# The low parts of the second attention's query weights on GpSimd instead of VectorE

## What is computed

```
for i in range(2):
    h = rms_norm(x, mix_norm[i])
    if i == 0: x = x + neighbourhood_attention(h, na_w_qkv, na_rpb, na_w_o)
    else:      x = x + sliding_window_gqa(h, swa_w_qkv, swa_sinks, t5_rel_table, swa_w_o)
    h = rms_norm(x, mlp_norm[i])
    x = x + relu(h @ mlp_w_in[i])**2 @ mlp_w_out[i]
return rms_norm(x, final_norm)
```

```
s = q @ k.T + bias            # within |i - j| <= 128
m = max(max(s), sink)
p = exp(s - m) / (sum(exp(s - m)) + exp(sink - m))
o = p @ v;  x = x + o @ w_o
```

## Time and profile before

| what | value |
|---|---|
| median of 3 runs | 1150.6 us (1150.18 to 1153.1) |
| the profiled execution | 1150.15 us |
| its span, first to last instruction | 1148.5 us |
| mean granted PE clock | 0.998 of full |
| PE busy | 1136.8 us, 99% of the span |
| DVE busy | 629.9 us, 55% |
| ACT busy | 504.9 us, 44% |
| POOL busy | 137.7 us, 12% |
| w_lo on DVE (line 1074) | 178 instructions, 1229 ns each on the mean |
| w_lo on POOL (line 335) | 2 instructions, 2388 ns each on the mean |
| second attention | about 598 to 750 us of the span |

### The profile page before, as it was taken

One profiled execution on the slowest core, in us unless ns is written; L12 is line 12 of the kernel. 1 busy time (PEld: TensorE's weight loads), 2 busy tenths in 40 slices (PEclk: granted clock), 3 DMA queues, 4 the chain that ended last, 5 costly groups with the idle time before them and its releaser, 6 DMA issues.

```text
span 1148.5 us, 16697 instructions
## 1 busy us (share of the span) xinstructions
PE 1136.8 (99%) x5648; PEld 938.1 (82%) x5648; DVE 629.9 (55%) x1020; ACT 504.9 (44%) x908; POOL 137.7 (12%) x239
## 2 busy tenths in 40 slices
PE   8999999999999999999999999999999999999997
PEld 6888888888888888888887878888888888888886
DVE  7778887764442234444345778766444223444333
ACT  6777777553431124333324666645343112333221
POOL 6544341240000000000000322100000000000000
PEclk9999999999999999999999999999999999999999
DMA  6332321333222322332222112122322332232222
GB/s 219 100 91 83 99 87 58 92 119 103 98 92 94 108 92 91 99 102 83 99 91 92 47 55 61 52 74 93 108 92 92 96 105 92 91 104 97 91 92 92
DMA packets 34291, 106.98 MB, mean 93 GB/s; under 512 B 5760, under 2 KB 8096, under 8 KB 34256
## 3 DMA queue, kind: packets, MB, share of 16 engines
q1 hardware_dynamic: 29344, 98.61, 26.0%
q0 software_dynamic: 4768, 7.90, 2.9%
q10 hardware_dynamic: 144, 0.02, 0.0%
HBM read 103.84 MB, written 2.67 MB: 93 GB/s over the span
## 4 chain that ended last, share of the span: by engine, by line
PE 98%; DVE 1%; DMA 0%; ACT 0%; issue 0%; DVEq 0%; ACTq 0%
PE acc L395 29%; PE acc L396 28%; PE acc L397 28%; PE s_ps L498 3%; PE om_ps L532 2%; PE pt_ps L702 2%; PE om_ps L556 1%; PE om_ps L528 1%; PE pt_ps L519 1%; PE om_ps L488 1%; PE s_ps L395 1%; PE s_ps L396 1%; PE s_ps L397 1%; DVE w_lo L1074 0%; DMA w_raw<-in_wstream 0%; PE om_ps L541 0%
## 5 line engine op out<-in xcount | busy, mean ns | idle before, releaser
L796 ACT CAST w_hi<-w_raw 128x1024 fp32r<-128x1024 f32 x180 | 189.1, 1051 | 405.1 <-PE acc L397 398.0
L395 PE MATMUL acc<-h_hi,w_hi 128*128 128x512 f32 x792 | 318.3, 402 | 0.7 <-DVE w_lo L1074 0.7
L397 PE MATMUL acc<-h_hi,w_lo 128*128 128x512 f32 x792 | 309.0, 390 | 0.0
L396 PE MATMUL acc<-h_lo,w_hi 128*128 128x512 f32 x792 | 308.9, 390 | 0.0
L1074 DVE TENSOR_TENSOR w_lo<-w_raw,w_hi 128x1024 fp32r<-128x1024 f32 x178 | 218.8, 1229 | 143.3 <-ACT w_hi L796 142.7
L395 PE MATMUL acc<-u_hi,w_hi 128*128 128x512 f32 (+1 forms) x624 | 241.3, 387 | 0.0
L397 PE MATMUL acc<-u_hi,w_lo 128*128 128x512 f32 (+1 forms) x624 | 239.5, 384 | 0.0
L396 PE MATMUL acc<-u_lo,w_hi 128*128 128x512 f32 (+1 forms) x624 | 239.5, 384 | 0.0
L395 PEld LDWEIGHTS acc<-h_hi,w_hi 128*128 128x128 f32 x792 | 148.7, 188 | 37.1 <-issue 4.2
L397 PEld LDWEIGHTS acc<-h_hi,w_lo 128*128 128x128 f32 x792 | 148.7, 188 | 31.7
L396 PEld LDWEIGHTS acc<-h_lo,w_hi 128*128 128x128 f32 x792 | 148.9, 188 | 28.3 <-issue 0.7
(11 more groups left out here) (135 smaller groups left out, 1019.3 us busy)
## 6 DMA issues: line engine op xcount, KB each, us to landing
w_raw<-in_wstream SPq DMA_DIRECT2D x180, 512.0 KB, 3.3
bias_pairs<-rpb_reversed POOLq DMA_DIRECT2D x64, 62.0 KB, 2.4
bias_pairs<-t_shifted POOLq DMA_DIRECT2D x64, 48.0 KB, 2.1
x_res<-in_xT SPq DMA_DIRECT2D x8, 256.0 KB, 5.7
out_y<-x_res SPq DMA_DIRECT2D x8, 128.0 KB, 1.8
out_y<-x_res SPq DMA_DIRECT2D x4, 256.0 KB, 2.3
t_shifted<-vT POOLq DMA_DIRECT2D x16, 31.0 KB, 2.1
mask<-in_mask POOLq DMA_DIRECT2D x1, 64.0 KB, 5.2
```

The lines of the kernel that those rows point to most:

```text
L395: nc.tensor.matmul(dst, a[0], b[0], start=start, stop=False)
L396: nc.tensor.matmul(dst, a[0], b[1], start=False, stop=False)
L397: return nc.tensor.matmul(dst, a[1], b[0], start=False, stop=stop)
L796: nc.scalar.copy(w_hi[:, c.odd, :], w_raw[:, c.odd, :]).then_inc(w_hi_made, 1)
```

## The change

POOL gets the low parts of chunks 102 to 109 (the query weights of the pairs 2 to 7 and the first two chunks of the output projection). For chunk 102 it does so ahead of its loop, for chunk 101 + p at the head of the turn in which it issues the bias loads of pair p, ahead of these, and for chunk 109 behind the loop. Each waits for ACT's cast and for the low part of the chunk before. DVE no longer makes them. In the last step DVE waits for the low part of chunk 109 before it makes that of chunk 110, so that `w_split` counts up in order. POOL's helper now takes the class `At`, whose `.v` is a number or a register's value.

```diff
@@ gpsimd
             def split_weights(c):
 
-                pool.wait_ge(w_hi_made, c + 1)
-                pool.wait_ge(w_split, c)
-                nc.gpsimd.tensor_tensor(w_lo[:, c % 2, :], w_raw[:, c % 2, :], f32(w_hi[:, c % 2, :]),
+                pool.wait_ge(w_hi_made, (c + 1).v)
+                pool.wait_ge(w_split, c.v)
+                nc.gpsimd.tensor_tensor(w_lo[:, c.odd, :], w_raw[:, c.odd, :], f32(w_hi[:, c.odd, :]),
                                         ALU.subtract).then_inc(w_split, 1)
@@
             for pair in range(2):
                 load_t5_bias(At(pair))
                 place_sinks(At(pair))
-            split_weights(CH_MLP0 + 2)
+            split_weights(At(CH_MLP0 + 2))
+            split_weights(At(CH_SW + 6))
             with pool.Fori(1, PAIRS // 2) as i:
                 for n in range(2):
                     pair = At(n, 2, i)
+                    split_weights(pair + (CH_SW + 5))
                     pool.wait_ge(probs_made, (pair * 4 + (UNITS_NA - 4)).v)
                     pool.wait_ge(esink_made, (pair * 2 + -2).v)
                     load_t5_bias(pair)
                     place_sinks(pair)
-            split_weights(CH_MLP1 + 2)
+            split_weights(At(CH_SW + PAIRS + 5))
+            split_weights(At(CH_MLP1 + 2))
@@ vector, sw_step
                     if before or n >= 1:
                         sw_pt_low(*sw_unit_by(p, n, -1))
-                    if n == 0:
-                        split_weights(m + (CH_SW + 5))
                     if n == 3 and not dense:
+                        dve.wait_ge(w_split, (m + (CH_SW + 6)).v)
                         split_weights(m + (CH_SW + 6))
```

## The result

The changed kernel takes 1152.36 us (median of 22 runs, 1151.44 to 1155.04), the kernel before in the same sessions 1150.46 us (22 runs, 1149.97 to 1153.1). The ratio is 1.0019, with a 95% interval of 1.0013 to 1.0025: the medians differ by 1.9 us, and the interval leaves out both no change and 0.3%. The profiled execution took 1151.83 us around a span of 1150.2 us; before it was 1150.15 around 1148.5. The two profiles differ by 1.7 us, nearly what the medians do, and can be held side by side.

The account below looks back on a forecast made before the run. The prediction took PE, busy for 99% of the span, as the bound. Parts 1 to 4 gave 0 and part 5 1.7 us: 1151.85 us against the profiled 1150.15, 1152.3 with the median's 0.45 us; range 1150.1 to 1154.2 us.

Parts of the forecast that it names:

- Part 1: Second attention's steps: DVE loses a 1.22 us subtraction in each of eight, 9.8 us in sum; booked 0.
- Its other end: Upper bound for relieving DVE in the eight steps: 1 us gained, from the weight-load shares.
- the share of the weight loads: PE's weight-load busy share: 80% in a step against 81% in the dense stage, at most about 1 us of slack.
- Part 2: Steps: POOL's 2.38 us subtraction readies the low part 1.5 us earlier, 6.4 us of cover before PE's need; price 0.
- Part 3: Steps: bias loads and two small copies queue behind POOL's work, with 3.5 us margin at the worst landing; price 0.
- Part 4: Last step: DVE's added wait is for a chunk POOL begins over 10 us ahead; price 0.
- Part 5: Stage start, before PE's first scores: POOL's chunk 102 subtraction holds DVE's u_lo, stalling PE 1.7 us (bounds 0 to 1.8).
- the tail of 0.54 us: First attention: u_lo ended 0.54 us behind POOL's bias addition; the same lag was applied at the second attention's start.
- (a): Stage start: DVE isn't held, or hardly; time stays 1150.6 us, or 1151.1; chance 0.22 together with (d).
- (b): Steps: faster because DVE was the hidden bound; up to 9.8 us go, 1140.8 us at the most; chance 0.03.
- (c): Every step: POOL holds DVE, 0.9 us in eight steps, 7.4 us, 1159.7 us with the start's stall; chance 0.04.
- (d): Stage start: POOL reaches its instruction late and misses DVE's u_lo; (a)'s time; chance 0.22 together with (a).

Follow-up runs that it names:

- the two kernels without the meeting: Changed kernel with chunk 102 given back to DVE, 1150.48 us; changed kernel with POOL waiting for DVE's low part of the last values before chunk 102, 1150.33 us.
- pieces: Changed kernel with POOL's subtraction for chunk 102 cut into four instructions of 256 columns; 1150.59 us, ratio 1.0002.
- copy: Changed kernel with chunk 102 on DVE and, at that moment, a POOL copy of 1024 columns on an unused tile; 1150.80 us, ratio 1.0003.
- long subtraction: Changed kernel with chunk 102 on DVE and, at that moment, a POOL subtraction of 2048 columns on an unused tile; 1155.27 us, ratio 1.0046.
- upper runs: The ten of the changed kernel's 22 runs above 1153 us, with a mean clock of 0.9963 against 0.9978 in the other twelve.
- The variant with the late chunk 102: Changed kernel, all eight chunks on POOL, but chunk 102 first waits for DVE's low part of the last values; 1150.33 us, ratio 0.9999.
- the kernel with chunk 102 alone: Kernel before with only chunk 102 moved to POOL, DVE keeping the other seven; 1151.89 us, ratio 1.0014.
- The four runs with the longer pause: Runs of the long subtraction kernel (2048 columns on POOL, unused tile, chunk 102 on DVE); median 1155.27 us.

## Why the prediction was right

The forecast was 1152.3 us, the result 1152.36, and the mechanism was the one stated: one hold ahead of the first step, nothing in the steps. By its parts:

- **Part 1, 0 for the relief of DVE.** Right: 0.93 us less to do in a step, 15.95 us a step. Its other end, 1 us gained, lies at the edge of the intervals of the two kernels without the meeting, so it is not strictly excluded; but both medians lie within 0.1 us of the kernel before. The starts of matmuls had been the better guide here than the share of the weight loads, which left 1% open.
- **Part 2.** POOL's 2.38 us and its lag of 0.09 us carried over: 2.37 to 2.39 us each. The next weight load was issued at 659.20 us, 3.67 us behind the cast's start; in the kernel before it was 659.20 as well, but 5.19 us behind the cast of its step. These are the 1.5 us earlier that were stated.
- **Part 3.** The bias loads began 3.45 us behind the cast's start instead of 0.86, the 2.6 us stated; no wait of DVE for them.
- **Part 4.** The added wait shows no idle time.
- **Part 5, the 1.7 us.** u_lo ended at 625.46 (625.49 stated), PE's first scores came 1.62 us later than before on the same scale (the trace of after runs 0.04 us ahead of the old one at that point), and the stretch lost 1.56 us of busy PE. The prediction read the tail of 0.54 us from a single meeting in the first attention; the other six there have 0.54 to 0.56 us as well. The step from instructions of 0.7 us to one of 2.4 us was the one not borne out by rows; the kernels with pieces, copy and long subtraction bear it out, each with an end of u_lo 0.55 us behind POOL's.
- **What the sum did not hold** is the clock. The rows before had it at full speed, and the pause was priced by its length alone. The median would be some 0.5 us lower without the upper runs (their twelve companions have a mean of 1151.87 us). That the forecast met the median to 0.1 us is in part luck: 1.55 to 1.6 us of pause in place of 1.7, 0.45 us from the median of only three runs before (by 22 runs it is 0.31), and a share of upper runs that was booked nowhere.
- **Rivals.** (a) fell by u_lo's 2.46 us, (b) by the unchanged steps, (c) by DVE's unchanged 0.42 and 0.69 us beside POOL, (d) by POOL's start 0.07 us behind the cast.

The variant with the late chunk 102 takes the loss away, but it only equals the kernel before. None of the kernels run here is faster than the kernel before beyond its interval.

## What to carry to other kernels

Before moving elementwise work to GpSimd, list for each instruction moved what VectorE does in those microseconds. If GpSimd's instruction reads SBUF, one with both inputs in SBUF was held to GpSimd's end (0.69 us became 2.46) or held it; one with an input from PSUM wasn't (0.42 us beside it). If the two must meet, let GpSimd wait for the other or cut its instruction in pieces; each took the loss away here. And relief of an engine that is busy for 81% of a step (12.93 of 16 us) was worth nothing, since the bound engine never lost a start to it: look at starts on the bound engine, and at the first turn of a pipelined stage by itself, where the cover of the later turns does not exist yet.

## What the runs showed of the hardware

- Behind a pause of 2.76 us on PE, which resumed at 627.35 us, the granted clock was 0.64 on the mean from 628 to 630 us, 0.50 from 630 to 632 and 1.00 from there; behind one of 1.55 to 1.56 us it was 1.00 in the four traces of the changed kernel and in that of the kernel with chunk 102 alone. The four runs with the longer pause had mean clocks of 0.994 to 0.996.
- A DVE instruction of 0.69 us that met a reading POOL instruction ended 0.54 to 0.56 us behind POOL's end, whether POOL's took 0.74, 1.05, 1.89, 2.39 or 3.60 us.
- POOL: 128x1024 subtraction 2.39 us, in four pieces 0.74, 1.18 (held), 0.72 and 0.73 us; in place on one tile 1.89 us, and 3.60 us for 2048 columns; a copy of 1024 columns 1.05 us; a fill of 2048 columns 1.81 us.
- The eight bias loads of the step shown were issued in 3.99 us after the change, against 4.75 us before; why is open, and nothing hung on it.
